# The norm's gain applied as a row ahead of the transposes, and the value transposes of fox's pairs moved behind the next pair's first scores

## The reference, cut to what matters

```python
def rmsnorm(x, g):
    y = x * lax.rsqrt(jnp.mean(x * x, axis=-1, keepdims=True) + EPS)
    return y * g                       # first step of all: h = rmsnorm(x, norm_g[0])

def fox_mixer(h, w_in, b_f, w_out):    # per head of 64 columns
    q, k, v, z = h @ w_in[q], h @ w_in[k], h @ w_in[v], h @ w_in[z]
    s = q k^T / 8 + c[t] - c[s]        # causal; c: running sum of log f
    o = softmax(s) v
    return (o * jax.nn.silu(z)) @ w_out
```

## Time and profile before

| what | us |
|---|---|
| median of three runs (2944.05 to 2948.44) | 2944.58 |
| the profiled execution | 2939.5 |
| its span | 2937.4 |
| PE busy in the span | 2820.5 (96%) |
| DVE, ACT, POOL busy | 1135.5, 899.6, 1023.9 |

### The profile page before, as it was taken

One profiled execution on the slowest core, in us unless ns is written; L12 is line 12 of the kernel. 1 busy time (PEld: TensorE's weight loads), 2 busy tenths in 40 slices (PEclk: granted clock), 3 DMA queues, 4 the chain that ended last, 5 costly groups with the idle time before them and its releaser, 6 DMA issues.

```text
span 2937.4 us, 39794 instructions
## 1 busy us (share of the span) xinstructions
PE 2820.5 (96%) x16428; PEld 2192.5 (75%) x16428; DVE 1135.5 (39%) x2501; ACT 899.6 (31%) x1693; POOL 1023.9 (35%) x443
## 2 busy tenths in 40 slices
PE   6979999899999999999999999999999999999998
PEld 4756676677677777776887878888888888887886
DVE  7998996556432223224345011111112111114323
ACT  4322323552333333334113122222222222224112
POOL 2532382143322222223541433333333333333541
PEclk8989999999999999999999999999999999999999
DMA  4100121121211111112221111111111111113211
GB/s 102 42 22 22 28 70 59 70 68 37 66 51 42 32 50 51 51 44 87 65 72 58 54 41 36 49 38 44 41 46 44 44 40 41 44 44 137 72 48 60
DMA packets 222367, 155.02 MB, mean 53 GB/s; under 512 B 26294, under 2 KB 209116, under 8 KB 222060
## 3 DMA queue, kind: packets, MB, share of 16 engines
q1 hardware_dynamic: 210220, 122.62, 14.6%
q10 hardware_dynamic: 11968, 29.87, 2.8%
HBM read 132.99 MB, written 19.47 MB: 52 GB/s over the span
## 4 chain that ended last, share of the span: by engine, by line
PE 86%; DVE 7%; ACT 3%; issue 3%; DMA 1%; POOL 1%; ACTq 0%; DVEq 0%; POOLq 0%
PE proj L890 21%; PE proj L892 21%; PE proj L891 21%; PE score L1185 3%; PE score L1200 3%; PE out L1215 3%; PE score L1334 1%; PE out L1387 1%; DVE arena L2261 1%; PE score L1364 1%; PE out L1392 1%; DVE arena L2263 1%; DMA y_scratch<-arena 1%; PE proj L919 1%; PE score L1343 1%
## 5 line engine op out<-in xcount | busy, mean ns | idle before, releaser
L890 PE MATMUL proj<-act_hi,w_hi 128*128 128x512 f32 x2560 | 1030.0, 402 | 14.3 <-ACT hT L1801 6.1
L892 PE MATMUL proj<-act_hi,w_lo 128*128 128x512 f32 x2560 | 1004.0, 392 | 0.0
L891 PE MATMUL proj<-act_lo,w_hi 128*128 128x512 f32 x2560 | 1003.2, 392 | 0.0
L763 POOL TENSOR_TENSOR w_hi<-w_raw,ones 128x1024 fp32r<-128x1024 f32 x177 | 425.2, 2402 | 1654.5 <-PE proj L892 1635.5
L890 PEld LDWEIGHTS proj<-act_hi,w_hi 128*128 128x128 f32 x2560 | 485.2, 190 | 126.9 <-issue 21.2
L892 PEld LDWEIGHTS proj<-act_hi,w_lo 128*128 128x128 f32 x2560 | 484.1, 189 | 104.5
L891 PEld LDWEIGHTS proj<-act_lo,w_hi 128*128 128x128 f32 x2560 | 485.5, 190 | 95.8 <-issue 0.2
L765 POOL TENSOR_TENSOR w_lo<-w_raw,w_hi 128x1024 fp32r<-128x1024 f32 x181 | 447.6, 2473 | 96.6 <-ACT w_hi L1961 82.7
L1801 ACT ACTIVATE arena<-proj 128x512 f32<-128x512 f32 x236 | 175.8, 753 | 682.5 <-PE proj L892 657.3
L2405 DVE SCALAR_TENSOR_TENSOR arena<-arena,score 128x256 f32<-128x256 f32 (+1 forms) x192 | 76.2, 428 | 721.0 <-PE score L1334 678.8
L2301 DVE CUSTOM_DVE_ANT_0 arena<-arena,score 128x512 f32<-128x512 f32 (+2 forms) x192 | 102.7, 573 | 368.1 <-PE score L1185 361.4
(11 more groups left out here) (260 smaller groups left out, 2855.9 us busy)
## 6 DMA issues: line engine op xcount, KB each, us to landing
w_raw<-dil_w_in_dram SPq DMA_DIRECT2D x80, 512.0 KB, 3.7
w_raw<-fox_w_in_dram SPq DMA_DIRECT2D x32, 512.0 KB, 4.2
w_raw<-w_in_dram SPq DMA_DIRECT2D x23, 512.0 KB, 3.8
y_scratch<-arena ACTq DMA_DIRECT2D x21, 512.0 KB, 4.0
act_lo<-y_scratch SPq DMA_DIRECT2D x21, 512.0 KB, 6.2
arena<-decay_scratch ACTq DMA_DIRECT2D x16, 512.0 KB, 6.7
w_raw<-ple_w_gate_dram SPq DMA_DIRECT2D x16, 512.0 KB, 3.9
arena<-x_dram SPq DMA_DIRECT2D x12, 512.0 KB, 5.5
```

The source lines that it names most:

```text
L763: pool.tensor_tensor(hi, raw, one.unsqueeze(1).broadcast_to([P, KB, P]), ALU.mult).then_inc(w_hi_done, 1)
L890: pe.matmul(bank, hi, a_hi, start=first, stop=False)
L891: pe.matmul(bank, hi, a_lo, start=False, stop=False)
L892: return pe.matmul(bank, lo, a_hi, start=False, stop=last)
```

## The change

In the start, the gain is loaded as a row of 1024 values, repeated on all 128 partitions (512 KB in place of 4 KB), on the same queue at the same place. DVE's scaling becomes a `scalar_tensor_tensor` that also multiplies by this row, ahead of the transposes. `gained` and `xg` are gone: ACT's copy and DVE's lower part read the transposed tile from `score` in PSUM, and PE's transposes of tile t wait for the lower part of tile t-2 in place of its gain product.

In the pairs of dsa and fox the pass X comes last: q, k, vT, g, X. Where a pair is projected on its own, the order is vT1, g0, g1, X0, X1. In dsa's second pair X0 stands at turn 4 and X1 at the end of turn 7. In fox's pairs 1 to 7 the X of a pair is made within the pair itself: X0 behind scores(0, 0), X1 behind scores(1, 0), and ACT evacuates both behind the store of the pair before. The waits at the pair's start leave X out, and PE waits for its evacuation ahead of the first values. SP's wait in `finished_rows` leaves it out for fox too.

```diff
-ORDER = dict(dsa="TTTXT", fox="TTTXT", dil="TTTTTTTTXTXTX")
-PAIR_ROLES = (("q", 0), ("k", 0), ("vT", 0), ("v", 0), ("g", 0))
+ORDER = dict(dsa="TTTTX", fox="TTTTX", dil="TTTTTTTTXTXTX")
+PAIR_ROLES = (("q", 0), ("k", 0), ("vT", 0), ("g", 0), ("v", 0))
...
-PAIR_HALVES = ((0, 0), (0, 1), (1, 0), (1, 1), (2, 0), (2, 1), (3, 0), (4, 0), (3, 1), (4, 1))
+PAIR_HALVES = ((0, 0), (0, 1), (1, 0), (1, 1), (2, 0), (2, 1), (3, 0), (3, 1), (4, 0), (4, 1))
...
     if kind == "fox":
-        n = t if t < 6 else t + 2
-        return ([unit(7)] if t == 6 else []), unit(n, 0), unit(n, 1), ([unit(6)] if t == 5 else [])
-    n = (4 if p == 0 else 8) + t // 4
-    turned = [unit(6 + t // 3)] if p == 1 and t in (0, 3) else []
-    return turned, (unit(n, t // 2 % 2) if t % 2 else None), None, []
+        return [], unit(t, 0), unit(t, 1), []
+    turned = [unit(8)] if p == 1 and t == 4 else []
+    return turned, (unit((4 if p == 0 else 6) + t // 4, t // 2 % 2) if t % 2 else None), None, ([unit(9)] if p == 1 and t == 7 else [])
+
+
+def turns_late(kind, p):
+    return kind == "fox" and p > 0
...
-        xg = A1.take(2 * T).rearrange("p (n c) -> p n c", n=2)
+        gain0_row = A1.take(T)
...
-                    sp.wait_ge(pass_done[half], base + PASSES[kind] * len(ORDER[kind]) - (1 if kind == "dil" else 0))
+                    sp.wait_ge(pass_done[half], base + PASSES[kind] * len(ORDER[kind]) - (0 if kind == "dsa" else 1))
...
                 pe.wait_ge(N0["xs"], t + 1)
-                wait(pe, N0["g"], t - 1)
+                wait(pe, N0["lo"], t - 1)
                 for k in range(KB):
                     mm = pe.transpose(score[:, t % 2, k * P:(k + 1) * P], xs[:, t % 2, k * P:(k + 1) * P], ident[:, :])
                 mm.then_inc(N0["tr"], 1)
...
-            pe.wait_ge(N0["g"], NT)
+            pe.wait_ge(N0["lo"], NT)
...
+                    late = turns_late(kind, p)
                     for half in range(2):
-                        pe.wait_ge(pass_free[half], p * NB + (first + NB))
+                        pe.wait_ge(pass_free[half], p * NB + (first + NB) - late)
                     scores(0, 0)
+                    if late:
+                        project(p, [(NB - 1, 0, None)])
                     if kind == "dsa" and p == 0:
                         project(2, [(b, half, None) for b, half in PAIR_HALVES[2:3]])
                     scores(1, 0)
+                    if late:
+                        project(p, [(NB - 1, 1, None)])
                     if kind == "dsa" and p == 0:
                         project(2, [(b, half, None) for b, half in PAIR_HALVES[3:4]])
                     if p > 0:
...
                         scores(i + 1, 1)
+                        if late and i == 0:
+                            for half in range(2):
+                                pe.wait_ge(pass_free[half], p * NB + (first + NB))
                         transposes(i, 1)
                         if follow:
                             if second_part is not None:
...
-            load_gain(act, 0).then_inc(gain_in, 16)
+            act.dma_start(gain0_row, a["norm_g"].broadcast_to([P, D])).then_inc(gain_in, 16)
...
-                act.wait_ge(N0["g"], t + 1)
-                act.activation(act_hi[:, :, t * P:(t + 1) * P], xg[:, t % 2].rearrange("p (k c) -> p k c", c=P),
+                act.wait_ge(N0["tr"], t + 1)
+                act.activation(act_hi[:, :, t * P:(t + 1) * P], score[:, t % 2].rearrange("p (k c) -> p k c", c=P),
                                ACT.Copy).then_inc(N0["hi"], 1)
...
                     if p > 0:
                         store(p - 1)
+                    late = turns_late(kind, p)
                     for half in range(2):
-                        act.wait_ge(pass_free[half], p * NB + (base + NB))
+                        act.wait_ge(pass_free[half], p * NB + (base + NB) - late)
+                    if late:
+                        projected(p, set_of(kind, p), [(NB - 1, half, None) for half in range(2)])
                     if follow:
                         decay(p + 1, 1 - turn_)
                     act.activation(R["e"], Q["g"], ACT.Tanh, scale=0.5).then_inc(S["gate"], 1)
...
-            def gained(t):
-
-                dve.wait_ge(N0["tr"], t + 1)
-                wait(dve, N0["lo"], t - 1)
-                wait(dve, N0["hi"], t - 1)
-                dve.tensor_tensor(xg[:, t % 2].rearrange("p (k c) -> p k c", c=P),
-                                  score[:, t % 2].rearrange("p (k c) -> p k c", c=P),
-                                  gains[:, 0].unsqueeze(2).broadcast_to([P, KB, P]), ALU.mult).then_inc(N0["g"], 1)
...
                 dve.wait_ge(N0["hi"], t + 1)
                 tok = slice(t * P, (t + 1) * P)
-                dve.tensor_tensor(act_lo[:, :, tok], xg[:, t % 2].rearrange("p (k c) -> p k c", c=P),
+                dve.tensor_tensor(act_lo[:, :, tok], score[:, t % 2].rearrange("p (k c) -> p k c", c=P),
                                   act_hi[:, :, tok].bitcast(F32), ALU.subtract).then_inc(N0["lo"], 1)
...
-                dve.tensor_scalar(xs[:, t % 2], xin[:, t], small[:, 2 * t + 1:2 * t + 2], None, ALU.mult).then_inc(N0["xs"], 1)
-                if t >= 1:
-                    gained(t - 1)
+                dve.scalar_tensor_tensor(xs[:, t % 2], xin[:, t], small[:, 2 * t + 1:2 * t + 2], gain0_row, ALU.mult, ALU.mult)\
+                   .then_inc(N0["xs"], 1)
                 if t >= 2:
                     low_parts(t - 2)
-            gained(NT - 1)
             low_parts(NT - 2)
             low_parts(NT - 1)
```

More of the change, by code:

```diff
@@ L532, in build @@
         XIN = [sem(f"x_moved{t}") for t in range(NT)]
-        N0 = sems("first", "sq root rstd xs tr g hi lo raw rev")
+        N0 = sems("first", "sq root rstd xs tr hi lo raw rev")
         SPLIT = sems("act_split", "in0 in1 in2 late hi lo")
```

## The result

The changed kernel takes 2950.89 us (median; 2946.25 to 2956.38), the kernel before 2944.91 beside it. The ratio is 1.0019, 95% interval 1.0013 to 1.0026: slower by 5.6 us, 3.8 to 7.7. The forecast was 2947.4, within 0.2% of no change; the measured difference stands at the upper edge of that band.

A forecast was written before the change was run, and what follows sets the result against it. TensorE (86% of the chain) was taken to bound the kernel, so edits pay only where it is late or starts earlier. Terms -4.1 - 1.6 - 0.7 + 2.0 + 7.8 - 0.6 = +2.8 on 2944.6 gave 2947.4 us, range 2938 to 2958.

The forecast's parts named there:

- The start: Before PE's first projection: early scaling and no gain product start PE at 30.7 instead of 34.82, -4.1 us.
- the seams: Six seams between fox's pairs: q waits about 1.7 us for ACT's X0 copy behind the store; +1.3 each, +7.8 us.
- The lock: At the start: POOL's split holds up DVE's two-SBUF-input scaling (2.26 us), not the PSUM-reading lower part (1.22); without it -7.1.
- rival 3: At the start: ACT sets the pace, PE starts at 27.7, -7.1 instead of -4.1 us, total 2944.4; chance 0.12.
- dsa's passes: Projections ahead of dsa's pairs: X waits saved, but POOL starts its windows later and PE waits for q; -0.7 us.
- the late turn: Ahead of dsa's pairs: the last turned output comes behind both halves of g, 4 us later, delaying POOL's windows.
- dsa's pairs: dsa's second pair: X0 in the scores' way, X1 ahead of the next pair's scores, later row loads; +2.0 us.
- The late loads: After dsa's second pair: loads of finished rows wait for X, about 3 us later; 0.7 us added.
- fox's first pair: Projections ahead of fox's first pair: with g ahead of X, waits and X shrink from 3.8 to 2.25; -1.6 us.
- rival 1: fox's seams: PE doesn't wait for X0's evacuation; -0.6 each, -3.5 instead of +7.8, total 2936.1 us; chance 0.13.
- fox's last pair: Seam of fox's last pair, no q behind it: first values wait 1.5 more, mostly absorbed; -0.6 us.
- Rival 2: fox's six seams: the 1.7 us wait takes PE's granted clock down, 10 us in all, total 2957.5; chance 0.12.

The follow-up runs named there:

- start_only: The kernel before with only the start changed (gain row in the scaling, no separate gain product); 2939.43 us, ratio 0.9985 to the kernel before.
- dsa_fill: The changed kernel with parts of g at turns 0, 2, 4, 6 of dsa's second pair and X1 heading turn 7; ratio 1.0015 to the kernel before.
- rows_early: The changed kernel with dsa's finished-row loads waiting for the last pass but one (g), no longer for X; ratio 1.0015 to the kernel before.
- late_all: The changed kernel with ACT's copies of X ahead of the store and fox's first pair treated like its others; 2936.25 us, ratio 0.9972 to the kernel before.
- evac_first: The changed kernel with ACT's copies of X0 and X1 ahead of the store in fox's pairs 1 to 7; 2940.87 us, ratio 0.9986 to the kernel before.

## Why the prediction was right, and where it wasn't

The total, +2.8 forecast and +5.6 (3.8 to 7.7) measured, was right within its range, but by terms that missed in both directions. The steps that belong to the change are -7.2 + 1.0 + 4.4 - 0.1 + 8.7 - 1.0 = +5.8. The start came out 3.1 below its forecast and the other terms together 6.1 above theirs: that the two half cancel, and the total stays in the range, is luck. The largest term, the seams, was right in its mechanism.

**Start: right in its mechanism, mis-sized (-4.1 against -7.2).** The lock was there: 2.06 to 2.95 us for the scaling beside a split over the 12 traces (2.26 taken), 1.21 for the lower part (1.22 taken). The rule that the prediction took from the Trainium skill (SBUF — State Buffer, section Who interferes with whom) is borne out on both: the scaling, with two SBUF inputs, is held up beside POOL's split, the lower part, which reads PSUM for one, is not. What I mis-sized is how many tiles it meets: the row landed 1.7 us earlier than the vector of before, POOL began its first split at 18.06 where it had begun at 17.07, and four scalings ran at 1.28 ahead of it, so that only two (2.37 and 2.06) stood ahead of the fourth lower part, where I had three. It ended at 25.9, not 28.7, and PE started at 27.68.

That is the time of rival 3, 27.7, but not its mechanism: ACT didn't set the pace, its copies of tiles 3 and 4 themselves waited 0.22 and 1.23 us for PE's transposes, which waited for DVE. The agreement is chance. POOL's split set it: the row landed at 9.8 to 10.4 us in the 12 traces, and the fifth scaling ended at 21.4 to 21.7 in all of them, 1.1 behind the end of POOL's first split. Behind the first projection the gain varies: at 93 us the 12 traces are 5.1 to 7.4 early. In the total, start_only's ratio gives -4.4 (-7.1 to -1.5), so that -7.2 is what one trace shows and not what the whole time is known to gain.

**dsa's passes: the wait was right, what follows it was not (-0.7 against +1.0).** POOL's idle 3.4 us for the late turn and PE's wait for q came as told. PE took q at 444.86 where before it did at 449.3; with the 3.75 us that the kernel was early at 383 this is the -0.7 forecast. The step that failed is that I counted a wait of 2.25 us at its own length. Behind it PE ran at half clock and lost another 1.6.

**dsa's pairs: mis-sized (+2.0 against +4.4).** The step is 4.4 in the changed kernel's first trace and 4.4 to 5.6 in five others that have this code there. "X0 moves from turn 0, where PE waited anyway" was priced at the 0.44 us that it costs elsewhere. With the new order the clock fell at this turn (2.1 us); dsa_fill shows that a filled turn 0 doesn't prevent it, so what in the order brings it stays open. The late loads cost 1.0 to 2.2 (rows_early), where I had 0.7.

**fox's first pair: the saving came and went (-1.6 against -0.1).** PE's first score comes 1.7 us nearer than in start_only, which has the old order; that is the -1.6. Behind it the clock fell and took as much; late_all, where it doesn't fall, keeps the saving.

**Seams: right (+1.3 against +1.45 each).** The wait of "about 1.7 us" is 1.66, six times, for the cause named. evac_first, which takes it away, lands at -0.46 a seam, near the -0.6 of rival 1. The part at the seam was forecast at +2.3 and is +2.32 (from 1024 to 1042 us of before); the part saved in the pair before was put at 1.03 and is 0.86.

**fox's last pair: right within its bounds (-0.6 against -1.0).** The wait of 2.34 is 3.71 there, 1.4 more where 1.5 was forecast. The clock over 1330 to 1360 is 0.94 where the kernel before has 0.89.

**Rival 2, the clock, was right in kind and in the wrong place.** At the seams the granted clock stayed at 1.00, at all 36 of the six traces that have this wait. It fell at three other places, for some 5 us in all, and this step was missing from the prediction: it let the clock fall only behind the seams. One of the two rows on which it weighed this was misread. The wait of 2.19 lies from 359.4 to 361.6, not within 361 to 363; the conclusion holds, since the clock is 1.00 over 359 to 366 too. The Trainium skill (TensorE: Matmul & The Clock Gate, section HAM oscillation) describes bursts of matmuls that each start at the lower clock behind a wait that recurs, there of some 3 to 5 us. Here no wait recurs in that way: a single one of 2.25 was followed by matmuls at half clock, one of 2.19 and 36 of 1.66 were not. The rows decide case by case.

## What to carry to other kernels

A pass moved into a wait frees nothing if its copy out of PSUM queues behind something that waits longer: read the order on the copying engine first, and put the copy ahead of the store. A short wait can cost more than its length: three reordered places lost the higher clock and paid 1.6 to 2.1 us beyond their waits, so look at the clock behind each place where work was moved. Work put into a wait didn't keep it up in dsa_fill; late_all kept it up, but moved the work both into a wait and away from ahead of one, and which of the two did it isn't shown. Before charging a difference between two traces to a change, profile the unchanged kernel twice: here equal code differed by 3.6 us.

## What the runs showed of the hardware

- A scaling with two SBUF inputs (scalar_tensor_tensor, 128x1024) took 1.28 us alone and 2.06 to 2.95 beside a GpSimd split (12 traces); a subtraction of the same size that reads one input from PSUM took 1.21 to 1.23 in both places.
- A single wait of 2.25 us, behind one of 0.25 and a set of transposes, was followed by matmuls at half clock (0.43 us apart instead of 0.23); a wait of 2.19 us straight behind matmuls was not, nor one of 1.66 us at 36 seams.
- Two waits of 0.89 and 0.75 us close together left the clock at 1.00 with 24 matmuls right ahead of them (the kernel before), and brought it to half for 3 us with a wait of 0.25 between two sets of transposes ahead of them.
- At a score behind a wait of 0.61 us the clock fell to half in all eight traces with one order of the passes and in none of the six with the other, and in the changed kernel it did so ahead of the next wait (1.21 us). No run here shows what decides it.
